# Attention scores from rounded parts stacked on 128 partitions, the mask added by the matrix engine, one row of 640 scores

## The reference, cut to what matters

```python
proj = hx @ w_in
q = proj[..., :Q_END]; k = ...; v = ...; u_gm, v_gm = split(gelu(proj[..., KV_END:]))
q, k = _apply_axial_rope(q, cos, sin), _apply_axial_rope(k, cos, sin)
# per block of 128 queries: the keys of three blocks and 256 context keys
mask = (abs(kpos - qpos) <= WINDOW) & (kpos >= 0) & (kpos < S)
s_loc = where(mask, einsum('bnqhgd,bnkhd->bnhgqk', qb, kb), NEG_INF)
s_ctx = einsum('bnqhgd,bchd->bnhgqc', qb, kc)
m = maximum(max(concatenate([s_loc, s_ctx])), sink)
p = exp(scores - m) / (sum(exp(scores - m)) + exp(sink - m))
out = p[..., :384] @ vb + p[..., 384:] @ vc
```

## Time and profile before

| | us |
|---|---|
| median of 3 runs | 4246.86 (4241.06 to 4252.22) |
| the profiled execution | 4251.61 |
| its span, first to last instruction | 4249.8 |
| projection, from its first matmul to its last | 98 to 272 |
| attention, from the first score to the last copy | 273 to 565 |
| PE busy over the span | 3722.0 (88%) |
| DVE, ACT busy | 2303.0 (54%), 1736.9 (41%) |
| mean granted clock of PE | 0.927 |

### The profile page before, as it was taken

The page is one execution under the profiler, slowest core; times in us unless marked ns, Lnnn a source line. Parts: engine busy times, 40 slices in busy tenths (PEclk is TensorE's granted clock), DMA queues, the critical chain, the costliest instruction groups (busy, mean ns, idle before and its releaser), DMA issues. The chain is left out here.

```text
span 4249.8 us, 60251 instructions
## 1 busy us (share of the span) xinstructions
PE 3722.0 (88%) x21778; PEld 3329.7 (78%) x21779; DVE 2303.0 (54%) x3130; ACT 1736.9 (41%) x2256; POOL 145.4 (3%) x171
## 2 busy tenths in 40 slices
PE   5988868899999956288999998997899999999993
PEld 3974437688888844268999998996799998999993
DVE  2337743344444442366655555555565598665665
ACT  5146622422322123265443334335544365444442
POOL 0000000000000020300000000000000000000001
PEclk8988879899999978599999999998999999999996
DMA  5126642433323142576554444447744466544554
GB/s 174 41 97 222 238 142 109 155 103 99 105 94 96 62 151 111 147 274 205 187 168 149 139 142 141 148 142 238 249 149 148 154 227 218 166 160 159 174 165 192
DMA packets 433614, 662.68 MB, mean 156 GB/s; under 512 B 33409, under 2 KB 348929, under 8 KB 433409
## 3 DMA queue, kind: packets, MB, share of 16 engines
q1 hardware_dynamic: 413170, 588.38, 41.4%
q0 software_dynamic: 15776, 55.61, 3.8%
q10 hardware_dynamic: 4464, 16.25, 1.0%
HBM read 600.91 MB, written 59.29 MB: 155 GB/s over the span
## 5 line engine op out<-in xcount | busy, mean ns | idle before, releaser
L2214 DVE TENSOR_TENSOR moe_gu_lo<-moe_raw_gu_lo,moe_gu_hi 128x2048 fp32r<-128x2048 f32 x254 | 580.4, 2285 | 135.2 <-ACT moe_gu_hi L2055 131.3
L2055 ACT ACTIVATE moe_gu_hi<-moe_raw_gu_lo 128x2048 fp32r<-128x2048 f32 x254 | 485.8, 1913 | 256.2 <-DMA moe_raw_gu_lo<-in_moe_w_gate 216.9
L1899 PE MATMUL moe_g<-moe_x,moe_gu_hi 128*128 128x336 f32 (+4 forms) x1344 | 416.6, 310 | 39.3 <-issue 24.5
L2270 DVE SCALAR_TENSOR_TENSOR moe_y_t<-moe_y,moe_cols,moe_y_t 128x288 f32<-128x288 f32 (+4 forms) x728 | 371.4, 535 | 100.7 <-PE moe_y L1901 100.2
L1900 PE MATMUL moe_g<-moe_x,moe_gu_hi 128*128 128x336 f32 (+4 forms) x1344 | 416.2, 310 | 0.0
L1901 PE MATMUL moe_g<-moe_x,moe_gu_lo 128*128 128x336 f32 (+4 forms) x1344 | 415.0, 309 | 0.0
L1899 PE MATMUL moe_y<-moe_h,moe_d_hi 128*128 128x336 f32 (+4 forms) x1344 | 412.2, 307 | 1.3 <-DVE moe_y_t L2270 1.2
L1900 PE MATMUL moe_u<-moe_x,moe_gu_hi 128*128 128x336 f32 (+4 forms) x1344 | 410.3, 305 | 0.0
L1900 PE MATMUL moe_y<-moe_h,moe_d_hi 128*128 128x336 f32 (+4 forms) x1344 | 410.2, 305 | 0.0
L1901 PE MATMUL moe_y<-moe_h,moe_d_lo 128*128 128x336 f32 (+4 forms) x1344 | 409.5, 305 | 0.0
L1901 PE MATMUL moe_u<-moe_x,moe_gu_lo 128*128 128x336 f32 (+4 forms) x1344 | 409.4, 305 | 0.0
(11 more groups left out here) (333 smaller groups left out, 7987.2 us busy)
## 6 DMA issues: line engine op xcount, KB each, us to landing
moe_raw_gu_lo<-in_moe_w_gate SPq DMA_DIRECT2D x127, 1024.0 KB
moe_raw_gu_lo<-in_moe_w_up SPq DMA_DIRECT2D x127, 1024.0 KB, 7.6
moe_raw_d_lo<-in_moe_w_down SPq DMA_DIRECT2D x126, 1024.0 KB, 4.9
att_w_mod<-in_w_ada SPq DMA_DIRECT2D x20, 2048.0 KB
scratch_y<-att_zeros SPq DMA_DIRECT2D x11, 2048.0 KB, 13.9
ffn_raw_gu_lo<-in_ffn_w_gate SPq DMA_DIRECT2D x22, 1024.0 KB
ffn_raw_gu_lo<-in_ffn_w_up SPq DMA_DIRECT2D x22, 1024.0 KB, 7.9
ffn_raw_d_lo<-in_ffn_w_down SPq DMA_DIRECT2D x22, 1024.0 KB, 4.9
```

Of the source, the lines that this page charges most:

```text
L1899: pe.matmul(bank[:, 0:width], wh, moving[:, 0, 0:width], start=start, stop=False)
L2055: act.activation(hi[par][:, :, :], raw[par][:, :, :], ACT.Copy).then_inc(rounded, 1)
L2214: dve.tensor_tensor(lo[par][:, :, :], raw[par][:, :, :], hi[par][:, :, :].bitcast(F), ALU.subtract).then_inc(split, 1)
L2270: dve.scalar_tensor_tensor(y_t[:, db, 0:cols], y_ps[db % 4][:, 0:cols], gate, y_t[:, db, 0:cols], ALU.mult, ALU.add).then_inc(y_added, 1)
```

## The change

In the projection each q head of 64 is split into a rounded upper part and its remainder, and the two are stacked on 128 partitions (`q_parts`); of each key head both parts are there too, each twice, one above the other (`k_parts`). So a unit has four transposes. Two float32r matmuls, one with the key's upper part, one with its lower, then give the full product. DVE makes the parts after the rotation. To find the room, `raw` now lies in the memory of `w_lo`, whose split is done in place; SP waits for the last matmul of the piece that used it. A q piece is one transfer.

In attention the mask is a third float32r matmul (identity by mask) onto the near scores. Far scores end one bank and near scores begin the next, so that DVE takes one maximum over up to 640 columns and ACT one exponential, one division and one copy. Mask and identity are rounded by ACT at the start. The zeros that SP writes are half as wide and sent twice.

```diff
@@ projection_phase
-        raw = [sb(f"raw{i}", [P, KD, W]) for i in range(2)]
-        w_lo = [sb(f"w_lo{i}", [P, KD, W], R) for i in range(2)]
+        def in_place(n, s):
+            raw = nc.alloc_sbuf_tensor_at(f"proj_raw_{n}", s, F, offset=nc.sbuf_base)
+            return sb(n, s, R), raw
+        w_lo, raw = zip(*(in_place(f"w_lo{i}", [P, KD, W]) for i in range(2)))
-                    sp.wait_ge(split, i - 1)
+                    sp.wait_ge(mm, last_unit[i - 2] + 1)
-                for j in range(2 if PIECES[UNITS[u][0]][0] == "q" else 1):
+                for j in range(4):
...
-                    rotate(u, t, 4, to[:, :]).then_inc(ready, 1)
+                    rotate(u, t, 4)
+                    whole = with_cos[:, :].rearrange("p (h f) -> p h f", h=4)
+                    upper, lower = (roped[n % 2].rearrange("p (h s f) -> p h s f", h=4, s=2)[:, :, s, :] for s in range(2))
+                    link(dve.tensor_copy(upper, whole))
+                    dve.tensor_tensor(lower, whole, upper.bitcast(F), ALU.subtract).then_inc(ready, 1)
@@ attention_phase
-            rows = dram["y"].rearrange("(a c p) d -> a p c d", p=P, c=TILES_PASS)
+            rows = dram["y"].rearrange("(a p c) (s d) -> a p (c s) d", p=P, c=TILES_PASS, s=2)
...
+                near, far = score_ps[s % 2][:, NEAR:NEAR + last - first], score_ps[s % 2][:, FAR:NEAR]
+                if s == 0:
+                    pe.wait_ge(made, 2)
                 if s >= 2:
-                    pe.wait_ge(masked_ok, s - 1)
-                    pe.wait_ge(far_exp, s - 1)
-                pe.matmul(near_ps[s % 2][:, 0:last - first], q, keep["k_t"][rows, first:last], start=True, stop=True)
-                pe.matmul(far_ps[s % 2][:, 0:CTX], q, keep["k_t"][rows, TX * P:TX * P + CTX], start=True, stop=True)\
-                  .then_inc(scored, 1)
+                    pe.wait_ge(exp_ok, s - 1)
+                for part in range(2):
+                    k = keep["k_parts"][:, 2 * side + part, :]
+                    pe.matmul(near, q, k[:, first:last], start=(part == 0), stop=False)
+                    pe.matmul(far, q, k[:, TX * P:TX * P + CTX], start=(part == 0), stop=(part == 1))
+                pe.matmul(near, ident_r[:, :], mask_r[:, at:at + last - first], start=False, stop=True).then_inc(scored, 1)
...
-                dve.tensor_tensor(masked[s % 2][:, 0:keys], near_ps[s % 2][:, 0:keys], mask[:, at:at + keys], ALU.add)\
-                   .then_inc(masked_ok, 1)
-                dve.reduce_max(top[:, h, 1:2], far_ps[s % 2][:, 0:CTX], AX.X)
-                dve.wait_ge(masked_ok, s + 1)
-                link(dve.reduce_max(top[:, h, 0:1], masked[s % 2][:, 0:keys], AX.X))
-                link(dve.tensor_tensor(top1[:, h:h + 1], top[:, h, 0:1], top[:, h, 1:2], ALU.max))
+                link(dve.reduce_max(top[:, h:h + 1], score_ps[s % 2][:, FAR:NEAR + last - first], AX.X))
...
-                act.activation(prob[b][:, 0:keys], masked[s % 2][:, 0:keys], ACT.Exp, bias=less,
-                               accum_out=sums[b][:, 0:1]).then_inc(near_exp, 1)
-                act.activation(prob[b][:, 3 * P:3 * P + CTX], far_ps[s % 2][:, 0:CTX], ACT.Exp, bias=less,
-                               accum_out=sums[b][:, 1:2]).then_inc(far_exp, 1)
+                act.activation(prob[b][:, 0:keys], score_ps[s % 2][:, FAR:FAR + keys], ACT.Exp, bias=less,
+                               accum_out=sums[b][:, :]).then_inc(exp_ok, 1)
```

More of the change, by code:

```diff
@@ L369, in loads @@
         def loads(i):
-            return 16 * sum(4 if PIECES[j][0] == "q" else 1 for j in range(i % 2, i + 1, 2))
+            return 16 * (i // 2 + 1)
         @block.tensor
@@ L549, in attention_phase @@
+        prob = [sb(f"prob{i}", [P, KEYS]) for i in range(3)]
         prob_t = [sb(f"prob_t{i}", [P, 3 + TC, GROUP, P]) for i in range(2)]
-        near_ps = [ps(f"near{i}", [P, 512]) for i in range(2)]
-        far_ps = [ps(f"far{i}", [P, 512]) for i in range(2)]
-        near_t, far_t = ps("near_t", [P, 512]), ps("far_t", [P, 512])
+        NEAR = 512
+        FAR = NEAR - CTX
+        score_ps = [ps(f"score{i}", [P, 1024]) for i in range(2)]
+        turn_ps = ps("turn", [P, 1024])
         out_ps = [ps(f"out{i}", [P, 512]) for i in range(2)]
-        ld, scored, masked_ok, far_top, chain, minus_ok, near_exp, far_exp = (
-            sem(n) for n in ("ld", "scored", "masked", "far_top", "chain", "minus", "near_exp", "far_exp"))
@@ L557, in attention_phase @@
-        near_turned, far_turned, near_copied, far_copied, valued, scaled, inverse_ok, written = (
-            sem(n) for n in ("near_t", "far_t", "near_c", "far_c", "valued", "scaled", "inverse_ok", "written"))
+        ld, made, scored, chain, minus_ok, exp_ok = (sem(n) for n in ("ld", "made", "scored", "chain", "minus", "exp"))
+        turned, copied, valued, scaled, inverse_ok, written = (
+            sem(n) for n in ("turned", "copied", "valued", "scaled", "inverse_ok", "written"))
         STEPS = [(n, h) for n in range(TX) for h in range(Q_HEADS)]
@@ L605, in score @@
                 n, h = STEPS[s]
[L606 to L615 removed]
+                first, last, at = band(n)
+                side = h // GROUP
+                near, far = score_ps[s % 2][:, NEAR:NEAR + last - first], score_ps[s % 2][:, FAR:NEAR]
+                if s == 0:
+                    pe.wait_ge(made, 2)
+                if s >= 2:
+                    pe.wait_ge(exp_ok, s - 1)
+                q = keep["q_parts"][:, h, n * P:(n + 1) * P]
+                for part in range(2):
[3 more added lines that the diff above has]
+                pe.matmul(near, ident_r[:, :], mask_r[:, at:at + last - first], start=False, stop=True).then_inc(scored, 1)
             def turn(s):
@@ L619, in turn @@
                 first, last, _ = band(n)
-                keys = last - first
-                b = s % 3
-                pe.wait_ge(scaled, 2 * s + 2)
+                pe.wait_ge(scaled, s + 1)
                 if s:
-                    pe.wait_ge(near_copied, s)
-                for j in range(keys // P):
-                    x = pe.transpose(near_t[:, j * P:(j + 1) * P], prob[b][:, j * P:(j + 1) * P], keep["ident"][:, :])
-                x.then_inc(near_turned, 1)
-                if s:
-                    pe.wait_ge(far_copied, s)
-                for j in range(TC):
-                    x = pe.transpose(far_t[:, j * P:(j + 1) * P], prob[b][:, (3 + j) * P:(4 + j) * P], keep["ident"][:, :])
-                x.then_inc(far_turned, 1)
+                    pe.wait_ge(copied, s)
+                for j in range((last - first + CTX) // P):
+                    x = pe.transpose(turn_ps[:, FAR + j * P:FAR + (j + 1) * P], prob[s % 3][:, j * P:(j + 1) * P],
+                                     keep["ident"][:, :])
+                x.then_inc(turned, 1)
             def value(g, quarter):
@@ L647, in value @@
                         pe.wait_ge(written, g - 1)
-                    pe.wait_ge(near_copied, (g + 1) * GROUP)
-                    pe.wait_ge(far_copied, (g + 1) * GROUP)
-                tiles = [(j, first // P + j) for j in range((last - first) // P)] + [(3 + j, TX + j) for j in range(TC)]
+                    pe.wait_ge(copied, (g + 1) * GROUP)
+                tiles = [(j, TX + j) for j in range(TC)] + [(TC + j, first // P + j) for j in range((last - first) // P)]
                 parts = [(odd, m) for odd in range(2) for m in range(len(tiles))]
@@ L740, in _ @@
         def _(act):
+            act.wait_ge(ld, 32)
+            act.activation(ident_r[:, :], keep["ident"][:, :], ACT.Copy).then_inc(made, 1)
+            act.activation(mask_r[:, :], prob[0][:, 0:3 * P], ACT.Copy).then_inc(made, 1)
             def exps(s):
@@ L759, in divide @@
                 first, last, _ = band(n)
-                b = s % 3
+                b, keys = s % 3, last - first + CTX
                 act.wait_ge(inverse_ok, s + 1)
-                act.wait_ge(near_exp, s + 1)
-                act.activation(prob[b][:, 0:last - first], prob[b][:, 0:last - first], ACT.Copy, scale=inverse[b][:, :])\
-                   .then_inc(scaled, 1)
-                act.wait_ge(far_exp, s + 1)
-                act.activation(prob[b][:, 3 * P:3 * P + CTX], prob[b][:, 3 * P:3 * P + CTX], ACT.Copy, scale=inverse[b][:, :])\
-                   .then_inc(scaled, 1)
+                act.wait_ge(exp_ok, s + 1)
+                act.activation(prob[b][:, 0:keys], prob[b][:, 0:keys], ACT.Copy, scale=inverse[b][:, :]).then_inc(scaled, 1)
             def copy_turned(s):
@@ L2433, in backbone @@
             keep["attn_cols"] = left.enter_context(nc.sbuf_tensor("attn_cols", [P, 4, KD], F))
-            keep["gate0"] = left.enter_context(nc.sbuf_tensor("gate0", [P, D], F))
             keep["c_silu"] = left.enter_context(nc.sbuf_tensor("c_silu", [P, 2, KD], F))
```

113 lines of the change are left out of this document (48 added, 65 removed).

## The result

The changed kernel takes 4196.62 us, the median of 4 runs (4192.27 to 4204.19), against 4248.3 us of the kernel before (4241.06 to 4252.22) beside it: 0.9877 of its time, 95% interval 0.9857 to 0.9898, so some 52 us less. Its profiled execution took 4196.86 us with a span of 4195.0. The prediction had 4222 and a range from 4197 to 4258: the direction held, the gain was about twice as large, and the time lies 0.4 us under the lower end of the range.

The account below looks back on a forecast made before the run. Attention was taken as bound by a cycle of waits among PE, DVE and ACT, the projection by PE. Attention -43, start +2.3, projection +16.2 give -24.5 us: 4222 against the median of 4246.9, range 4197 to 4258.

Parts of the forecast that it names:

- the stalls: Projection: PE idles at unit 1's transposes of q0, q1 and kv, 2.8, 2.3 and 2.1 us, 7.2 in all.
- the falls of the clock: Projection: each of three PE gaps may lower the clock, costing 0 to 5 us; half, 2.5, was taken.
- The copy with rounding: Projection, DVE's new f32 copy: 0.25 or 0.43 us, the latter taken; 0.2 us in each of three stalls.
- The chain behind the late load: Projection, q0: next weights land 5.1 us after issue, ACT rounds 1.9, DVE subtracts 2.29 ahead of unit 1's rotation.
- The fixed prices of the attention step: Attention at full clock: scores 1.09 us, reduction of 640 columns 0.80, exponential about 0.77, giving 3.50 a step.
- The case that the wide read is no cheaper: Attention rival: 640-column reduction and exponential cost what their two parts did; 3.65 us a step, 4235 total; chance 0.07.
- The start: Start of attention: PE must wait until ACT has rounded mask and identity, losing 2.3 us.
- the step shortens by as much, so I expect the same share: Attention: PE's streamed columns fall with step length, so 30% of the time stays at the lower clock; 3.81 us a step.
- the factor 1.027: Attention: measured 4.61 us a step over the 4.49 worked out for both clocks; applied to 3.81, giving 3.91.
- the ring: Attention: cycle of waits among PE, DVE and ACT, advancing two steps a round; 7.98 us before, 6.69 after, 3.35 a step.
- the clock stays up: Attention rival: PE no longer idles long enough, all steps run at 3.59 us; total 4206; chance 0.15.
- the clock falls: Attention rival: fewer streamed columns and a colder engine; slower by over 0.3% above low share 0.88, up to 4269; chance 0.11.

Follow-up runs that it names:

- The second profile: Another profiled execution of the unaltered changed kernel, from its repeat beside the kernel before: 4205.51 us against 4256.34, ratio 0.9889.
- filling alone: Kernel before plus one unread matmul of 256 f32 columns per attention step, where PE waits for ACT's copy: 4228.98 us against 4256.34, ratio 0.9949.
- the second set of runs: The unaltered changed kernel measured again beside the kernel before: 4205.51 us against 4256.34, ratio 0.9889.
- the fills: Unread matmuls in PE's waits: kernel before, ratio 0.9949; changed kernel, 0.9898; changed kernel with two more exponentials a step, 0.9992 (4298.1 us against 4254.78 without them).

## Why the prediction was right and wrong, point by point

*The projection* came out at its +16.2 us, partly by luck: the stalls are 0.9 us less than predicted and the falls of the clock 0.9 more. Stalls 6.3 for 7.2: 2.28 us for 2.8, 2.49 for 2.3 and 1.48 for 2.1. Two falls of the clock, 3.4 us each at half speed, cost 3.4 us for 2.5. That leaves 6.5 for the transposes, as worked out. The second profile has 7.5 us of stalls and 17.4 us for the whole (173.3 to 190.7). A unit takes 3.31 us (3.30 predicted). The copy with rounding, with two prices open, takes 0.29 us for 256 columns, near the lower one; that is 0.14 us of each stall, and the rest of their misses stays unexplained. The chain behind the late load was right: DVE's subtraction started 7.1 us behind q0's first matmul (125.7 to 132.8), and 7.2 had been worked out (with 0.2 us between the issue and 5.1 us of load that the text does not name).

*The fixed prices of the attention step* held: reduction, exponential and scores within 0.03 us, and the step at the full clock 3.49 for 3.50. The case that the wide read is no cheaper fell with the forms' rows. The DMA queues did not bind, at a share of 0.82. The start lost 1.7 us for the 2.3 (9.1 us from the projection's last matmul to ACT's first step, where it was 7.4).

*The step that failed* is "the step shortens by as much, so I expect the same share". It kept 30% at the lower clock and so made 3.91 of 3.50. In the 48 steps the share was none. PE's streamed columns per time, from which it was argued, was the wrong quantity: by the prediction's own numbers they hardly moved (2.67 of 4.14 us and 2.29 of 3.50, 64% and 65%), while PE's idling shrank. Its one long idle stretch per round went from 1.66 to 1.15 us, since DVE and ACT had each lost three instructions a step, and its busy share at the full clock rose from 76 to 81%. That idling shrinks could have been had from the sum's own terms. PE's work in a round of two steps was twice 0.67 and twice 1.38, and two value quarters, 1.43 us for the one of three matmuls (six rows) and 1.00 for the one of two: 6.53 us of a round of 8.28, so 1.75 idle. In the changed kernel it is 5.95 (scores of 1.09) of 7.00, so 1.05 idle. That this would be enough to keep the clock up, the terms could not say. The price: predicted were 3.91 us a step, measured are 3.48, 0.43 less. Of that 0.31 is the clock's share (3.81 for 3.50), 0.10 the factor 1.027, which belonged to the mixture and not to the full clock, and 0.02 the ring. 0.43 x 48 = 21 of the missing 25 us; the other 4 lie in the start and the other steps, 10.5 us shorter for the 6.7 of the sum. By the measured paces the change saves 1.15 us a step (4.63 to 3.48), and the runs split this: by filling alone, without any shorter ring, the kernel before gets 0.48 of them (4.63 to 4.15), the change's shorter ring the other 0.67.

*The rival "the clock stays up"* is what happened. Its 4206 had kept the factor 1.027 (3.59 us a step for 3.48, 5 us in 48 steps); the other 4 to 5 us to the measured 4197 are of the size by which the untouched phases differ between two executions. In the second set of runs the ratio was 0.9889, which is 4200 on the prediction's 4246.9.

*The rival "the clock falls"* went by the streamed columns too: it feared that fewer of them chill the engine. What the fills changed is PE's idling. The Trainium skill, "TensorE: Matmul & The Clock Gate", section "A second HAM failure mode: psum-queue depth-cycling", tells of a kernel in which PE idled shortly but often between groups of matmuls and the clock went back and forth. This case agrees: in the kernel before it fell 16 times behind stretches of 1.05 to 1.71 us, and was up again 3.4 or 6.8 us later. In the changed kernel's attention it stayed up behind stretches of 1.0 to 1.24 us and one of 1.64, but for the one fall of its second profile.

Left open: whether the clock goes by the single stretch or by the idling summed over a stretch of time, for the fills and the change shortened both; two of the 16 falls in the kernel before came behind stretches of 1.05 and 1.23 us, as long as some that did no harm in the changed one. That the fill also helps in the later stages, which are at the lower clock for part of the time, was not tried.

## What to carry to other kernels

Where the granted clock is under 1 in a stage that is bound by a ring of waits, read PE's idle brackets on the timeline before carrying the clock's share over to the changed kernel: an edit that shortens the other engines' part of the ring can be worth its own time and the whole low share. Whether it is so can be tested in one run, with a matmul that nobody reads in PE's wait; if it pays, it may stay. Compare an engine's busy share only between stretches at the same clock, since at the lower one its own work swells. And cost both halves of a two-stage change apart: here the splitting gave in attention about what it took in the projection.

## What the runs showed of the hardware that was not expected

- One matmul of 256 f32 columns more per step made a kernel 22 us faster (0.9949), by lifting the granted clock from 0.82 to 1.00; in a kernel at the full clock it cost nothing and gave nothing.
- In the kernel before the clock fell behind idle stretches of PE as short as 1.05 to 1.71 us, with PE busy 76% of the time at the full clock; in other kernels stretches of 1.64, 1.83 and 2.07 us had no fall behind them.
- A reduction and an activation whose 640 columns of PSUM cross a bank edge cost what the columns give: 0.822 and 0.776 us.
- The f32 copy with rounding takes 0.29 us for 256 columns, where the two-operand subtraction takes 0.43.
- Scores over 64 partitions are no faster than scores over 128: 388 and 391 ns for a matmul of 384 columns, a step of 3.55 and 3.48 us (one profile of the former).
